# A hybrid attention and state-space decoder step: the order of the sample attention, an early load, and value pages laid as 32 rows of four keys

## The reference, cut to what matters

```python
past_s = gather_pages(cache_kv_sel[l], page_table)      # 16 pages of 128 keys per sequence
full_s = jnp.concatenate([kvs_past, kvs], axis=1)
...
ls = einsum(q, k_sel) * scale - slopes * dist_s         # selected blocks of 64 keys
ps = masked_softmax(ls)                                 # over the chosen blocks
o_s = einsum(ps, v_sel)
...                                                     # the same for the window: o_w
o = gate[0] * o_c + gate[1] * o_s + gate[2] * o_w
```

## Time and profile before

| | |
|---|---|
| runs, median (lowest to highest) | 2387.05 us (2383.47 to 2388.6) |
| profiled execution, its time | 2381.55 us |
| its span, first to last instruction | 2379.9 us |
| sample attention in it | 756.65 to 868.15 us |
| TensorE busy over the span | 93% |
| mean granted TensorE clock | 0.952 |

### The profile page before, as it was taken

The page is one execution under the profiler, slowest core; times in us unless marked ns, Lnnn a source line. Parts: engine busy times, 40 slices in busy tenths (PEclk is TensorE's granted clock), DMA queues, the critical chain, the costliest instruction groups (busy, mean ns, idle before and its releaser), DMA issues.

```text
span 2379.9 us, 33633 instructions
## 1 busy us (share of the span) xinstructions
PE 2221.3 (93%) x11942; PEld 1751.5 (74%) x11942; DVE 1347.8 (57%) x2179; ACT 513.3 (22%) x1191; POOL 781.1 (33%) x665
## 2 busy tenths in 40 slices
PE   8999899998898679999999999998788999999999
PEld 7867777876565458888887787886455788888877
DVE  4447878655895135556631278785766445566412
ACT  1202112004675212111100132332542011111000
POOL 3322000003002743443424345543663343343242
PEclk8999999996899789999999999998988999999999
DMA  4234442404003962612212221221430212212022
GB/s 166 71 107 136 121 136 87 127 14 142 27 2 122 346 232 72 230 71 81 86 65 91 92 71 71 90 74 39 177 124 18 98 44 99 78 71 91 29 98 86
DMA packets 87879, 237.10 MB, mean 100 GB/s; under 512 B 11457, under 2 KB 60738, under 8 KB 73378
## 3 DMA queue, kind: packets, MB, share of 16 engines
q1 hardware_dynamic: 66866, 192.48, 22.7%
q0 software_dynamic: 7024, 29.90, 3.8%
q10 hardware_dynamic: 13824, 12.59, 1.7%
HBM read 218.46 MB, written 23.73 MB: 102 GB/s over the span
## 4 chain that ended last, share of the span: by engine, by line
PE 72%; DVE 14%; issue 5%; POOL 3%; ACT 2%; POOLq 1%; SPq 1%; ACTq 1%; DMA 1%; DVEq 0%
PE ps L342 56%; PE ps L986 5%; POOL sbuf L3085 1%; PE ps L1489 1%; PE ps L1522 1%; PE ps L1502 1%; DVE sbuf L2468 1%; PE ps L1372 1%; POOLq L1778 1%; ACT sbuf L1577 1%; PE ps L897 1%; SPq L824 1%; PE ps L2658 1%; PE ps L469 1%; PE ps L549 1%
## 5 line engine op out<-in xcount | busy, mean ns | idle before, releaser
L342 PE MATMUL ps<-sbuf 128*128 128x272 f32 x6048 | 1412.0, 396 | 26.0 <-issue 8.9
L342 PEld LDWEIGHTS ps<-sbuf 128*128 128x128 f32 x6048 | 1155.4, 192 | 280.2 <-issue 15.6
L392 POOL TENSOR_TENSOR sbuf<-sbuf 128x512 f32<-128x512 f32 (+2 forms) x90 | 135.6, 1506 | 743.3 <-PE ps L342 552.5
L361 ACT ACTIVATE sbuf<-ps 128x272 f32<-128x272 f32 x180 | 71.5, 397 | 1118.4 <-PE ps L342 1084.1
L986 PE MATMUL ps<-sbuf 128*128 128x256 f32 (+1 forms) x1280 | 299.6, 393 | 5.6 <-ACT sbuf L1064 4.5
L986 PEld LDWEIGHTS ps<-sbuf 128*128 128x128 f32 x1280 | 244.6, 192 | 58.4 <-issue 5.9
L372 DVE TENSOR_TENSOR sbuf<-sbuf,ps 128x272 f32<-128x272 f32 x90 | 39.4, 437 | 256.0 <-PE ps L342 255.0
L401 POOL TENSOR_TENSOR sbuf<-sbuf 128x512 f32<-128x512 f32 (+2 forms) x90 | 141.8, 1576 | 7.8 <-PE ps L342 0.9
L398 POOL TENSOR_TENSOR sbuf<-sbuf 128x512 f32<-128x512 f32 (+2 forms) x90 | 136.4, 1515 | 12.2 <-DVE sbuf L409 5.3
L393 POOL TENSOR_TENSOR sbuf<-sbuf 128x512 f32<-128x512 f32 (+2 forms) x90 | 134.5, 1494 | 7.0
L380 DVE TENSOR_TENSOR sbuf<-sbuf,ps 128x272 f32<-128x272 f32 x90 | 39.4, 438 | 126.5 <-PE ps L342 125.7
(11 more groups left out here) (362 smaller groups left out, 2325.9 us busy)
## 6 DMA issues: line engine op xcount, KB each, us to landing
sbuf<-w_gu SPq DMA_DIRECT2D x44, 1024.0 KB, 4.9
sbuf<-w_down SPq DMA_DIRECT2D x32, 704.0 KB, 5.4
sbuf<-cmp_pages SPq DMA_DIRECT2D x160, 128.0 KB, 2.4
sbuf<-w_ssd_in SPq DMA_DIRECT2D x20, 1024.0 KB, 4.8
sbuf<-cmp_pages ACTq DMA_DIRECT2D x96, 128.0 KB, 3.6
sbuf<-w_nsa_in SPq DMA_DIRECT2D x9, 1024.0 KB, 4.8
sbuf<-sel_k SPq DMA_DIRECT2D x64, 128.0 KB, 2.8
sbuf<-sel_v SPq DMA_DIRECT2D x64, 128.0 KB, 4.0
```

The costliest lines, as they stand in the source:

```text
L342: last = pe.matmul(ps[:, bank_of(u, j), 0:HALF], a[:, kt * P:(kt + 1) * P], b[:, kt], start=kt == 0, stop=kt == kts - 1)
L361: do(act.activation(dst, bank_in(u, j), ACT.Copy), f_copied)
L392: do(pool.tensor_tensor(sv[:, 0], a21, a22, ALU.add), f_sums)
```

## The change

**Order.** TensorE makes the scores of pair pr+1 between the turning and the values of pair pr. For this each part of a pair gets its own banks: the weights are turned through banks 0, 1, 2, 3 and 5 and the window's through 4 and 5, without waits between them; the values go to bank 6 and the turned result to bank 7. The result of a pair is turned after the window weights of the next. VectorE and ScalarE follow: biases and exponentials of pair pr+1 come before the combining of pair pr.

**Loads.** 12 of the 16 pages of K3 are issued by POOL in the stage before; the other four come in this stage, ahead of mask(0). The order and the waits of all other loads stay.

**Layout.** A value page is loaded as 32 rows of 4 KB (four keys on a partition), and four pages lie on four quarters of the partitions. To match, the weights are turned from every fourth column of `S`.

```diff
+        SIXTH_EARLY = 12
 ...
+            p4_load_unit(pool, "K", 3, 0, SIXTH_EARLY)
 ...
+        TURN_BANK = (0, 1, 2, 3, 5)
+        def p4_load_unit(sp, kind, b, i0=0, i1=NPAGE):
+            rows = P // 4
+                pages[0:1, b * NPAGE + i0:b * NPAGE + i1], engines=[sp.engine], min_val=0, max_val=NPHYS - 1)
+            for i, page in enumerate(numbers, i0):
+                if kind == "V":
+                    sp.dma_start(UNIT[place(kind, b)][(i % 4) * rows:(i % 4 + 1) * rows, i // 4 * 1024:(i // 4 + 1) * 1024],
+                                 src[bass.ds(page, 1)].rearrange("o (r j) n -> (o r) (j n)", r=rows)
+                                 ).then_inc(unit_in[place(kind, b)], 16)
+                    continue
                 sp.dma_start(dst[:, i:i + 1], src[bass.ds(page, 1)].rearrange("o p n -> p o n")
 ...
             def scores(pr):
-                if pr >= 1:
-                    pe.wait_ge(ss_s, pr)
-                    pe.wait_ge(sw_s, pr)
                 for j in range(4):
+                    if pr >= 1:
+                        pe.wait_ge(ss_pt, 5 * (pr - 1) + j + 1)
 ...
             def turn(pr):
                 pe.wait_ge(ss_e, pr + 1)
                 for k, (j0, j1) in enumerate(TURNS):
-                    if k >= 2:
-                        pe.wait_ge(ss_pt, 5 * pr + k - 1)
-                    else:
-                        pe.wait_ge(sw_pt, 2 * pr + k + 1)
+                    if k == 4:
+                        pe.wait_ge(sw_pt, 2 * pr + 2)
                     for j in range(j0, j1):
-                        last = pe.transpose(ps[0:n, 6 + k % 2, ...], S[:, j * P:j * P + n], ident)
+                        at = j // 4 * 4 * P + j % 4
+                        cols = S[:, at:at + 4 * P:4] if j < NPAGE else S[:, PAST:PAST + NS]
+                        last = pe.transpose(ps[0:n, TURN_BANK[k], ...], cols, ident)
 ...
             for pr in range(PAIRS):
+                win_turn(pr)
+                if pr >= 1:
+                    turn_out(pr - 1)
                 turn(pr)
-                values(pr)
-                turn_out(pr)
                 if pr + 1 < PAIRS:
                     scores(pr + 1)
                     win_scores(pr + 1)
+                values(pr)
+            turn_out(PAIRS - 1)
 ...
+            p4_load_unit(pool, "K", 3, SIXTH_EARLY, NPAGE)
             mask(0)
-            p4_load_unit(pool, "K", 3)
```

More of the change, by code:

```diff
@@ L1288, in build @@
         vtok = region(2 * QT * 256).rearrange("p (b i n) -> p b i n", b=2, i=QT)
+        low = region(3 * 3 * 4).rearrange("p (w s x) -> p w s x", w=3, s=3)
+        PTc = region(2 * 4 * P).rearrange("p (x k n) -> p x k n", x=2, k=4)
+        vcP = region(4 * P).rearrange("p (q n) -> p q n", q=4)
+        SIXTH_EARLY = 12
+        sixth_at = phase_base + FT * NT + 3 * (FT // 2) * HALF
+        assert top[0] <= sixth_at
+        top[0] = sixth_at + SIXTH_EARLY * 256
         S_ring = region(S_BUFS * SEQ).rearrange("p (s n) -> p s n", s=S_BUFS)
         PT_ring = region(8 * SEQ).rearrange("p (s x n) -> p s x n", s=2, x=4)
-        low = region(3 * 3 * 4).rearrange("p (w s x) -> p w s x", w=3, s=3)
         cmp_small = region(4 * HEADS).rearrange("p (w h) -> p w h", w=4)
-        PTc = region(2 * 4 * P).rearrange("p (x k n) -> p x k n", x=2, k=4)
-        vcP = region(4 * P).rearrange("p (q n) -> p q n", q=4)
         Sc = rstd[:, 0:HEADS * 32]
@@ L1836, in win_scores @@
                 if pr >= 1:
-                    pe.wait_ge(ss_sum, pr)
+                    pe.wait_ge(sw_pt, 2 * pr)
+                    pe.wait_ge(ss_pt, 5 * pr)
                 pe.wait_ge(wk_in, 32 * (pr + 1))
@@ L1842, in win_scores, with win_turn, turn @@
                 last.then_inc(sw_mm, 1)
[L1844 to L1848, removed]
+            def win_turn(pr):
                 pe.wait_ge(sw_e, pr + 1)
                 for j in range(4):
-                    last = pe.transpose(ps[:, 6, j * P:(j + 1) * P], Sw[:, j * P:(j + 1) * P], ident)
+                    last = pe.transpose(ps[:, 4, j * P:(j + 1) * P], Sw[:, j * P:(j + 1) * P], ident)
                 last.then_inc(sw_t, 1)
-                pe.transpose(ps[0:NS, 7, 0:P], Sw[:, SEQ:SEQ + NS], ident).then_inc(sw_t, 1)
+                pe.transpose(ps[0:NS, 5, 0:P], Sw[:, SEQ:SEQ + NS], ident).then_inc(sw_t, 1)
+            def turn(pr):
                 pe.wait_ge(ss_e, pr + 1)
                 for k, (j0, j1) in enumerate(TURNS):
-                    if k >= 2:
-                        pe.wait_ge(ss_pt, 5 * pr + k - 1)
-                    else:
-                        pe.wait_ge(sw_pt, 2 * pr + k + 1)
+                    if k == 4:
+                        pe.wait_ge(sw_pt, 2 * pr + 2)
                     n = P if k < 4 else NS
                     for j in range(j0, j1):
-                        last = pe.transpose(ps[0:n, 6 + k % 2, (j - j0) * P:(j - j0 + 1) * P], S[:, j * P:j * P + n], ident)
+                        at = j // 4 * 4 * P + j % 4
+                        cols = S[:, at:at + 4 * P:4] if j < NPAGE else S[:, PAST:PAST + NS]
+                        last = pe.transpose(ps[0:n, TURN_BANK[k], (j - j0) * P:(j - j0 + 1) * P], cols, ident)
                     last.then_inc(ss_t, 1)
@@ L1867, in values @@
                 pe.wait_ge(ss_pt, 5 * pr + 5)
+                if pr >= 1:
+                    pe.wait_ge(ss_sum, pr)
                 for bb in range(2):
@@ L1874, in put @@
                         r, c = rows32(bb, gp), slice(gp * P, (gp + 1) * P)
-                        last = pe.matmul(ps[r, 5, col * P:(col + 1) * P], weights[:, r], rows(bb)[:, c],
+                        last = pe.matmul(ps[r, 6, col * P:(col + 1) * P], weights[:, r], rows(bb)[:, c],
                                          start=first, stop=end)
@@ L1888, in turn_out @@
                 pe.wait_ge(ss_sum, pr + 1)
+                if pr >= 1:
+                    pe.wait_ge(ss_o, 4 * pr)
                 pe.transpose(ps[:, 7, 0:P], o_rows, ident).then_inc(ss_ot, 1)
@@ L1906, in p4_act, with exps @@
             act.wait_ge(s_comb, 1)
-            for pr in range(PAIRS):
+            def exps(pr):
                 act.wait_ge(sw_s, pr + 1)
@@ L1934, in p4_act @@
                                        ACT.Copy).then_inc(ss_o, 1)
+            exps(0)
+            for pr in range(PAIRS):
+                take_turned(pr)
+                if pr >= 1:
+                    take_out(pr - 1)
+                if pr + 1 < PAIRS:
+                    exps(pr + 1)
+            take_out(PAIRS - 1)
             act.wait_ge(ss_o, 4 * PAIRS)
@@ L1942, in p4_dve, with biased @@
             S_in = ps.rearrange("p b n -> p (b n)")
-            for pr in range(PAIRS):
-                g = gate_rows[:, pr]
+            one = lambda w, pr: few[:, w, pr:pr + 1]
+            def biased(pr):
                 tail = cl_("tail")[:, pr * NS:(pr + 1) * NS]
-                one = lambda w: few[:, w, pr:pr + 1]
                 dve.wait_ge(ss_mm, pr + 1)
@@ L1952, in p4_dve @@
                 do(dve.tensor_tensor_reduce(Sw[:, SEQ:SEQ + NS], ps[:, 4, NS:2 * NS], tail, -1.0, 3e38, ALU.add,
-                                            ALU.min, one(3)))
+                                            ALU.min, one(3, pr)))
                 do(dve.tensor_tensor_reduce(S[:, PAST:PAST + NS], ps[:, 4, 0:NS], tail, -1.0, 3e38, ALU.add,
-                                            ALU.min, one(7)))
+                                            ALU.min, one(7, pr)))
                 dve.wait_ge(sw_mm, pr + 1)
[L1957 to L1960, removed]
+                dve.tensor_tensor_reduce(Sw[:, 0:SEQ], ps[:, 5], cl_("ali_w"), -1.0, one(3, pr), ALU.add, ALU.min,
+                                         one(4, pr)).then_inc(sw_s, 1)
+                dve.tensor_tensor_reduce(S[:, 0:PAST], S_in[:, 0:PAST], comb, -1.0, one(7, pr), ALU.add, ALU.min,
+                                         one(8, pr)).then_inc(ss_s, 1)
+            biased(0)
+            for pr in range(PAIRS):
+                g = gate_rows[:, pr]
                 dve.wait_ge(sw_e, pr + 1)
                 dve.wait_ge(ss_e, pr + 1)
[L1963 to L1966, removed]
+                do(dve.reciprocal(one(6, pr), one(5, pr)))
+                do(dve.reciprocal(one(10, pr), one(9, pr)))
+                do(dve.tensor_tensor(one(6, pr), one(6, pr), g[:, 2:3], ALU.mult))
+                do(dve.tensor_tensor(one(10, pr), one(10, pr), g[:, 1:2], ALU.mult))
+                if pr + 1 < PAIRS:
+                    biased(pr + 1)
                 dve.wait_ge(ss_pv, pr + 1)
@@ L1969, in p4_dve @@
                     dve.wait_ge(ss_ot, pr)
-                do(dve.tensor_scalar(o_rows, ps[:, 5, P:2 * P], one(6), None, ALU.mult))
-                do(dve.scalar_tensor_tensor(o_rows, ps[:, 5, 2 * P:3 * P], one(10), o_rows, ALU.mult, ALU.add))
-                do(dve.tensor_tensor(o_rows, o_rows, ps[:, 5, 0:P], ALU.add), ss_sum)
```

(3 more changed lines are left out.)

14 lines of the change are left out of this document (7 added, 7 removed).

## The result

| | before | after |
|---|---|---|
| runs, median (lowest to highest), five each | 2387.05 us (2383.21 to 2389.92) | 2400.86 us (2396.02 to 2401.49) |
| profiled execution, its span | 2379.9 us | 2399.2 us |
| mean granted TensorE clock | 0.952 | 0.950 |
| sample attention | 756.65 to 868.15 us | 754.99 to 883.65 us |

The changed kernel takes 1.007 times as long, with a 95% interval of 1.0052 to 1.0089. That is a small loss, but the whole interval lies above 1. At the median of about 2382 us that the kernel before had in the runs of the experiments it is 16.7 us (12.4 to 21.2); the two medians of the table lie 13.8 us apart. The 2400.86 us are above the predicted range. The stage grew from 111.5 to 128.7 us. It begins 1.7 us earlier and ends 15.5 later; the span of this one execution is 19.3 longer, so about 3.8 us more are lost behind the stage.

A forecast was written before the change was run, and what follows sets the result against it. POOL's queue was taken to bound the sample attention, with the loop replacing it after the change. Loop +4.2, value DMAs -0.8, turning -0.4 and stepped loads +0.3 gave +3.3 us, so 2390.4 us; range 2381 to 2397.

The forecast's parts named there:

- the loop: Sample attention: keys, scores, values, keys replace POOL's queue as the bound; K7's first DMA 4.2 us late.
- the turning: TensorE's transposes of the weights: two 0.23 us pauses between groups go, once on the path in the tail, -0.4 us.
- the layout: 32-row value pages: cheaper POOL DMAs give -0.8 us on V7, stepped weight loads add 0.3 us.
- first case: The forecast: keys, scores, values, keys set the sample attention's time; 2390.4 us, own range 2387 to 2393.5; chance 0.55.
- Only V6 and V7 can come late, and they have from 849 to 862; I take nothing: Value-page transfers in 32 rows: only the last two value units could be late; no time added.
- fourth case: Value units move at half rate, 168 GB/s, delaying the last units and window values; 2395.7 us; chance 0.08.
- K6 and K7 fill the gaps: Argument against half-rate value units costing time: the last two key units fill the gaps in the transfers.
- second case: POOL's queue stays the bound if values(1) end by 814.7 us; 2385.5 us; chance 0.17.
- third case: The transfers were the bound, so fewer bytes and larger packets make the stage faster; 2378.3 us; chance 0.13.
- fifth case: TensorE's weight loads from every fourth column take twice as long in the turning; 2396.5 us; chance 0.07.
- 32-row DMAs on POOL: POOL's issue of value pages gets 0.05 us a DMA cheaper, -0.8 us on V7.
- The head: Start of POOL's queue: K3 early takes 10.2 us off it, lost again at K5's wait for values(0).

## Why the prediction was wrong, point by point

**The sum.** The forecast was +3.3 us: the loop and the turning +3.8 (4.2 less 0.4), the layout -0.5 (-0.8 and +0.3). The runs gave +16.7: +7.4 without the layout (1.0031), and 9.3 more with it. Both parts were taken too small, and the layout by more.

**The loop (first case): right in mechanism, too small in size.** Its waits are there: POOL idle before K5 and K7, TensorE waiting 18.07 and 18.67 us for `sel_k`, no unit or mask outside the ring that sets it. Its times are not: K5, K7 and the end of mask(3) were to come at 791.5, 822 to 827 and about 851, and came at 795.89, 835.23 and 862.49. With 128-row pages they are nearer: 790.41, 826.92 and 854.29. K7 lies there inside its bound of 827.5, but the time of +7.4 us (5.2 to 9.8) is about twice the +3.8, and its middle lies just above what the low and high terms allow without the layout (+0.4 to +7.0). Term by term:

| term | forecast | kernel after | 128 rows |
|---|---|---|---|
| values(0) end | 786.2 | 790.1 | 784.6 |
| K4 and K5 issued | 800.9 | 805.2 | 800.0 |
| last key page to scores(2) | 4.9 | 6.5 | 6.2 |
| scores(2) | 5.9 | 6.30 | 6.60 |
| values(1), with its pause | 6.2 | 10.9 | 7.9 |
| K7, first DMA | 824.3 | 835.23 | 826.92 |

(A value run is taken from its start to the next instruction of TensorE; 4.43 us of the 10.9 and 3.23 of values(0) are pauses "issue".) The landing was too short because I took a median of all pages, where the last page of a burst decides. Between the two right columns K7 differs by 8.3 us. Most of it is in three parts, the rest nearly cancels. The pauses are 4.95 (3.23 + 4.43 against 0.20 + 2.51), the products behind them 2.4 (3.07 for 55 and 3.07 for 64 against 1.73 and 1.96), and values(0) begins 1.1 later, at 780.06 against 778.97. In the kernel before the pause of values(1) was 1.39. Behind the longer pause the granted clock was 0.53, the level of 1.2 GHz, where behind the one of 0.20 it was 1.00. Busy time by stretches, the kernel after and then the one with 128 rows:

```profile
787.00:790.00 3.00, 2.94 (x55) 2.73 (x54) 0.00 (x0) 0.00 (x0) 0.00 (x0) 0.53 0.06 18
```

```profile
782.90:784.60 1.70, 1.66 (x55) 1.46 (x54) 0.00 (x0) 1.70 (x1) 0.00 (x0) 1.00 0.11 31
```

The last two numbers of each row also show how far the loop empties the transfers: 0.06 of the engines' time while TensorE finishes the values that everything waits for.

What the pauses are is argued, not shown. In windows of 0.25 us the profile has a packet of the instruction queue at 784.6 and 823.9 us in the kernel after, at 780.6 and 817.1 in the one with 128 rows, and TensorE resumes 2.3 to 2.9 us behind each of the four, at the same product of the run in both kernels. The packets are 4.0 and 6.8 us later in the kernel after, and TensorE resumes 4.1 and 7.2 later. They share the engines with the value pages, so slow pages could make them late; no run moved the one without the other.

**The step that failed** is "Only V6 and V7 can come late, and they have from 849 to 862; I take nothing", and with it the fourth case at 0.08. The effect of the layout on the transfers was put at nothing, and measured 9.3 us on top of the loop (1.0070 less 1.0031, with an uncertainty of about 5 us); the case itself had 5.3. It priced slow value units by their own landing and that of the last window values. No values waited for a value unit, as it said; its sign, values(3) behind a wait for `win`, did come (2.31 us). The larger part of the price came through what shares the engines with the value pages: the pauses above and the slower products behind them in the kernel after, and with the layout alone window values(2) (11.04 us) and the issue of other units from SP's queue (15.47 and 26.56 us). And the rates were less bad than its half (168 GB/s): 249 to 265. The argument against it, "K6 and K7 fill the gaps", was wrong: with the layout alone there were no gaps, and SP was held at K6 with V6 behind it in the queue; in the kernel after there were gaps, and the loop had made them. The Trainium skill's rule on ports ("SBUF — State Buffer", Door 1: The DMA port swizzle) stood in the prediction with its sign, and was given too little weight, since no row showed such a load.

**POOL's queue stays the bound (second case)**: fell, 12.10 us of idle time before K7. It would have held with the values first, where K7 has 1.20.

**The transfers as the bound (third case)**: fell in its form, faster. With 128 rows the same bytes are out of the stage and the rate is 346 GB/s, and the stage still ends 5.7 us later than before.

**Stepped weight loads (fifth case)**: fell. Contiguous and stepped loads of a turning, from the kernel with 128 rows and the kernel after:

```profile
770.63 3.41 PEld L1868 LDWEIGHTS ps<-sbuf 128*128 128x128 f32 x17 [2.62 <-ACT sbuf L1927]
785.91 1.84 PEld L1868 LDWEIGHTS ps<-sbuf 128*128 128x128 f32 x17
```

```profile
771.25 3.42 PEld L1876 LDWEIGHTS ps<-sbuf 128*128 128x128 f32 x17 [2.62 <-ACT sbuf L1935]
791.36 2.03 PEld L1876 LDWEIGHTS ps<-sbuf 128*128 128x128 f32 x17
```

The step costs 0.01 us in turn(0), at a granted clock of 0.50, and 0.19 in turn(1), at 1.00, which TensorE spends before a wait for keys anyway. In turn(3) the loads take 3.40 against 3.31. So on the path it is about 0.1, and the 0.3 taken was more than enough.

**32-row DMAs on POOL**: 9.15 us for V7 against 9.32, so 0.01 us a DMA and not 0.05; of the -0.8, -0.17 came.

**The head and the turning**: K3 early cost nothing that shows in the stage before, and its gain was lost at K5 as foretold. By runs it is -0.12% (interval up to zero) alone. The tail from the end of mask(3) is 21.2 us against 20.7; with 128 rows it is 19.5. So the new order of the tail gave 1.2, more than the 0.4 taken; which part of it (the turning without waits, the earlier combining) no run tells. The wait for the window values (2.31 us) took it back.

**Behind the stage** I had taken no change. In the kernel after the output weights land later, so POOL's preparation of the next stage falls on VectorE's:

```profile
876.90 1.27 POOL L392 TENSOR_TENSOR sbuf<-sbuf 128x512 f32<-128x512 f32 x1 [14.41 <-DMA sbuf<-w_nsa_out]
...
883.63 2.42 POOL L393 TENSOR_TENSOR sbuf<-sbuf 128x512 f32<-128x512 f32 x1
...
884.96 2.24 DVE L407 TENSOR_TENSOR sbuf<-sbuf 128x1088 f32<-128x1088 f32 x1
```

Alone they take 1.27 and 1.29 us. Three such VectorE instructions make 2.8 us, and TensorE waits 1.94 for the second of them at 889.52. This is half of the 3.8 us, by the timelines of one execution; the rest is open, and may be chance: the same difference is 1.8 us with 128 rows and -1.3 with the order alone, where at most one pair of these instructions overlaps. No run took the overlap away alone.

**What stays open**: why pages on opposite halves reach 261 to 268 GB/s and not the 345 of pages on all rows; how much of the pauses in the values is the slow pages' doing; and whether order and layout share their waiting. The layout alone measured 0.92%, the whole change 0.70%, which the intervals don't part. Open is also why the layout alone costs more than the layout with values first (0.92% to 0.48%, clear of the noise), which has the early load and the new banks besides.

## What to carry to other kernels

Walk a reordered loop as a ring, buffer free to load to compute to buffer free, before counting what the head saves: POOL's queue, which had no free moment, stood idle for 18.45 and 12.10 us, because the values that it waits for stood behind the next scores, from pair 1 on behind scores that needed the keys still to be loaded. Price a slower transfer not by its own landing alone but by everything that shares its engines and its queue: window rows, the units issued behind it and, as far as the timelines tell, instructions. Keep such pages on all 128 rows: fewer rows gave next to nothing back on the issuing engine (0.17 us a unit), and none of the four orders of the pages that were run gave the rate back.

## What the runs showed of the hardware that I had not expected

- The rate of the value pages hung on which half of the partitions was written: 208 to 215 GB/s with both queues on one half, 261 to 268 on opposite halves, 345 with all 128 rows.
- 64 rows of 2 KB are no faster than 32 rows of 4 KB: 249 GB/s in both.
- SP's issue of 16 DMAs of 128 KB went from 8.63 us to 26.56 and 23.88 behind 32-row value pages in the two kernels with the values first; POOL's stayed at 9.33 in both.
- On POOL a DMA of 128 KB costs 0.57 us of queue (9.15 for 16) in 32 rows and 0.58 in 128.
- `tensor_tensor` on VectorE and on POOL at one time: 2.24 and 2.42 us in place of 1.29 and 1.27.
